# One block ahead: who writes the low parts of the expert weights in the selection stage

## What is computed

```python
q = (xb @ w_query).reshape(PEER_BLOCK, PEER_HEADS, 2, PEER_HALF)
s = jnp.einsum('bhpd,phnd->bhpn', q, sub_keys).astype(jnp.float32)
top_s, top_i = lax.top_k(s, PEER_TOPK)
cand = top_s[:, :, 0, :, None] + top_s[:, :, 1, None, :]
best_s, best_j = lax.top_k(cand.reshape(PEER_BLOCK, PEER_HEADS, PEER_TOPK * PEER_TOPK), PEER_TOPK)
...
eid = e1 * PEER_NKEYS + e2
gate = jax.nn.softmax(best_s, axis=-1)
act = jax.nn.gelu(jnp.einsum('bd,bhkd->bhk', xb, u_sel).astype(jnp.float32), approximate=False)
return jnp.einsum('bhk,bhkd->bd', (gate * act).astype(xb.dtype), v_sel)
```

## Time and profile before

| | us |
|---|---|
| median of 3 runs | 3571.84 (3567.01 to 3573.65) |
| profiled execution | 3573.65 |
| its span | 3572.0 |
| TensorE busy in the span (weight loads) | 3399.5 (3332.6) |
| VectorE busy | 2595.8 |
| ScalarE busy | 1021.5 |
| GpSimd busy | 978.6 |

### The profile page before, as it was taken

The page is one execution under the profiler, slowest core; times in us unless marked ns, Lnnn a source line. Parts: engine busy times, 40 slices in busy tenths (PEclk is TensorE's granted clock), DMA queues, the critical chain, the costliest instruction groups (busy, mean ns, idle before and its releaser), DMA issues.

```text
span 3572.0 us, 57535 instructions
## 1 busy us (share of the span) xinstructions
PE 3399.5 (95%) x21552; PEld 3332.6 (93%) x21552; DVE 2595.8 (73%) x5013; ACT 1021.5 (29%) x1355; POOL 978.6 (27%) x773
## 2 busy tenths in 40 slices
PE   6989999899998999999999899999999999999997
PEld 6989999879998999998898799999999999999996
DVE  5554344233343269999998999999999999999996
ACT  5742222121232233222454222222222222222222
POOL 0000000000000021111000655555555555555550
PEclk9999999879999999999999899999999999999998
DMA  2111111111232233333788999999899999989992
GB/s 107 36 34 37 47 39 37 49 48 47 76 119 75 84 102 113 104 106 105 218 266 275 358 322 327 338 329 322 322 327 328 334 331 326 325 319 332 326 325 108
DMA packets 304343, 698.60 MB, mean 196 GB/s; under 512 B 23856, under 2 KB 124208, under 8 KB 303184
## 3 DMA queue, kind: packets, MB, share of 16 engines
q0 software_dynamic: 98592, 362.97, 27.8%
q1 hardware_dynamic: 104112, 276.89, 22.6%
q10 hardware_dynamic: 101504, 56.89, 5.2%
HBM read 604.44 MB, written 92.22 MB: 195 GB/s over the span
## 4 chain that ended last, share of the span: by engine, by line
PE 78%; DVE 16%; DVEq 2%; issue 2%; DMA 1%; ACT 1%; ACTq 0%; POOL 0%; SPq 0%; PEldq 0%; POOLq 0%
PE PS L1454 28%; PE PS L366 16%; PE PS L1437 14%; PE PS L1158 7%; PE PS L1187 5%; DVE HOTG L1944 3%; PE PS L1369 3%; DVE HOT L1940 1%; PE PS L381 1%; DVE HOT L1941 1%; DVE fold L1872 1%; DVE besti L1816 1%; DVE sc L1807 1%; DVE besti L1808 1%; DVEq L1870 1%
## 5 line engine op out<-in xcount | busy, mean ns | idle before, releaser
L1454 PE MATMUL PS<-AH,VH 128*128 128x368 f32 x2048 | 515.5, 333 | 17.6 <-DVE AL L2042 12.6
L1454 PE MATMUL PS<-AH,VL 128*128 128x368 f32 x2048 | 516.4, 333 | 0.0
L1454 PE MATMUL PS<-AL,VH 128*128 128x368 f32 x2048 | 511.0, 331 | 0.0
L715 POOL DMA_INDIRECT SLOT<-rows_u,EID x256 | 346.9, 1355 | 598.4 <-DMA GW<-gate_matrices 293.0
L715 POOL DMA_INDIRECT SLOT<-rows_v,EID x256 | 333.2, 1301 | 203.4 <-DVE SLOT L1974 164.6
L1454 PEld LDWEIGHTS PS<-AH,VH 128*128 128x128 f32 x2048 | 366.5, 189 | 20.0 <-DVE AL L2042 13.5
L1454 PEld LDWEIGHTS PS<-AL,VH 128*128 128x128 f32 x2048 | 367.6, 189 | 0.0
L1454 PEld LDWEIGHTS PS<-AH,VL 128*128 128x128 f32 x2048 | 366.8, 189 | 0.0
L1983 DVE SCALAR_TENSOR_TENSOR XLF<-SLOT,GA,XLF 128x1024 f32<-128x1024 f32 x256 | 327.5, 1279 | 1.3 <-DMA SLOT<-rows_v,EID 1.1
L1044 ACT ACTIVATE VH<-VRAW 128x512 fp32r<-128x512 f32 x256 | 157.6, 628 | 567.2 <-PE PS L1454 567.2
L1974 DVE SCALAR_TENSOR_TENSOR SLOT<-SLOT,XHF 128x1024 f32<-128x1024 f32 x256 | 311.9, 1219 | 6.2 <-DMA SLOT<-rows_u,EID 6.2
(11 more groups left out here) (332 smaller groups left out, 6559.4 us busy)
## 6 DMA issues: line engine op xcount, KB each, us to landing
RAW<-experts_u SPq DMA_DIRECT2D x128, 512.0 KB, 6.0
VRAW<-experts_v SPq DMA_DIRECT2D x256, 256.0 KB, 5.7
gate_matrices<-stg ACTq DMA_DIRECT2D x22, 2048.0 KB, 10.3
GW<-gate_matrices SPq DMA_DIRECT2D x96, 384.0 KB, 6.8
RAW<-weights SPq DMA_DIRECT2D x69, 512.0 KB, 3.5
activations<-AS SPq DMA_DIRECT2D x64, 368.0 KB, 2.5
AS<-activations SPq DMA_DIRECT2D x64, 368.0 KB, 3.0
GW<-gate_matrices SPq DMA_DIRECT2D x32, 320.0 KB, 5.8
```

Source lines behind the costliest of these rows:

```text
L715: pool.indirect_dma_start(out=SLOT[n % NSLOT][:, :], out_offset=None, in_=table, in_offset=bass.IndirectOffsetOnAxis(ap=ids, axis=0)).then ...
L1454: mm = pe.matmul(PS[:, 4 + 2 * (d % 2) + t, 0:CH], w[:, d % 2, c * P:c * P + P], x[:, c, t * CH:t * CH + CH], start=(c == 0 and n == 0), s ...
```

## The change

GpSimd writes one more low part before tile 0 (blocks 0 to 3 in place of 0 to 2), and in the tiles +2, +3 and +4 in place of +1, +2 and +3. Its load of `qst` still stands behind the first of them. VectorE writes +5 and +6 in place of +4 and +5. Its first low part stands where it stood. The second stands ahead of the product with `second`, where it was behind it, and in the last tile there is none. The orders of TensorE, ScalarE and SyncE are the same as before.

```diff
-            for n in range(1, PRE + 1):
+            for n in range(1, PRE + 2):
                 e_low(n, n % 2)
...
-                e_low(FIRST_E[i] + 1, (FIRST_E[i] + 1) % 2)
+                e_low(FIRST_E[i] + 2, FIRST_E[i] % 2)
...
-                for r in range(2, SEL_E[i] - 1):
+                for r in range(3, SEL_E[i]):
                     e_low(FIRST_E[i] + r, (FIRST_E[i] + r) % 2)
...
                 dve.tensor_tensor(hot[:, :, :, :], places(topf), names(startb), ALU.is_ge)
-                e_low(FIRST_E[i + 1] - 1)
+                e_low(FIRST_E[i + 1])
...
                 dve.tensor_tensor(hot[:, :, :, :], places(topf), names(iota_b), ALU.is_equal)
+                if i + 1 < NTILE:
+                    e_low(FIRST_E[i + 1] + 1)
                 dve.drain()
                 dve.tensor_tensor(by_head(pick), by_head(hot), values(second), ALU.mult)
-                e_low(FIRST_E[i + 1])
                 fold(e2)
```

## The result

The change makes the kernel slower: 3619.51 us (median of 4 runs, 3618.04 to 3621.10) against 3572.52 for the kernel before on the same chip. The ratio is 1.0135, with a 95% interval of 1.0117 to 1.0152. That is 47.0 us more where 32.3 were forecast, and outside the range of 3588 to 3614. The direction and the place were right; the size was not.

What follows compares the result with a forecast made beforehand. VectorE's stream was taken as the clock from tile 2 on, TensorE in tiles 0 and 1. Terms 11.7 + 1.7 + 2.5 + 0.5 + 9.4 + 5.3 + 1.2 = 32.3 us gave 3604 us, range 3588 to 3614.

Steps and rivals of the forecast that it cites:

- steady tile: Tiles 4, 5 and 7: length from tick to tick grows from 47.65 to 50.9 us, taken as 3.15 a tile.
- rival 1: TensorE is the bound and its waits on VectorE's low parts go: about 3558 us; chance 4%.
- A: VectorE's early low-part place, L1781 after `hot` of L1877; forecast 3.25 us of new idle time before it in steady tiles.
- late place: VectorE's second low-part place in a tile; claimed to cost nothing more, with cover of 0.8 us a tile.
- block +3 ends at +32.75: TensorE, steady tile: start of scores to end of block +3 takes 19.70 us, so high part +5 is there at +35.9.
- lead in tiles 4 to 7: How far TensorE is ahead there; could be worse or better by 0.8 us a tile, ±3 in the sum.
- B: VectorE's late low-part place, reached at +45.3; high part +6 forecast near +44.5, 0.2 us of cost in tile 2.
- `qst` term: Tile 0: load queued behind GpSimd's first low part, so scores start at 1307.5 instead of 1304.40: 3.1 us of TensorE lost.
- Tile 6's growth: Tile 6 loses its short cast of `besti` (0.29 us) as the reason for 45.25 us and becomes about 50.6: 5.3 us.
- low part beside `hot`: GpSimd's low part +4 beside `hot` of L1877, 2.40 us alone, 2.55 beside VectorE's work: 0 to +0.8 in tiles 2 and 8.
- Rival 3: Only the early tiles pay; TensorE gets ahead after tile 3: 16.4 less 1.2 us, 3587; chance 10%.
- Rival 4: More than the sum: B's cover gone and `qst` late, 1 to 1.5 us more in each of eight tiles: 3615; chance 9%.

Runs made afterwards that it cites:

- fastest kernel of the study: Kernel before, but GpSimd writes +1 to +4, VectorE only +5 ahead of the product, and the exponential stands behind the fourth block: 3563.95 us.
- same kernel with the early exponential: Kernel before, but GpSimd writes +1 to +4 and VectorE only +5 ahead of the product; exponential left behind the third block: 3576.17 us.
- clock held: Changed kernel with useless matmuls in TensorE's wait before the scores: 3611.86 us; the 51.02 of tile 6 has them before block +4 too: 3610.29 us.
- first fillings: Changed kernel with useless matmuls on TensorE where it stands before the scores of tiles 1 to 8: 3611.86 us.
- both waits are filled: Changed kernel with useless matmuls on TensorE before the scores and also before the last block of a tile: 3610.29 us.

## Why the prediction was right and wrong

**Where it was right.** VectorE sets the pace in the steady tiles, and rival 1 (TensorE as the bound) fell: its waits for `WL` went away here, and the kernel is slower. The fastest kernel of the study has 1.22 us less on VectorE in each tile, and VectorE runs without a gap through its tiles 4 to 7; so it does in the same kernel with the early exponential, where the product of 3.2 us makes them 2 us longer. A waits nine times, seven of them for ScalarE's `WH` and two for GpSimd's low part +4 (4.5 us, tiles 2 and 8). The scores' starts (+13.03 forecast +13.05; in tile 0 1307.39 for 1307.5), the 3.03 us on ScalarE, the 14.9 us behind A in tile 5, and the free late place in tiles 4 to 6 all came as worked out. With the clock held, the steady tile is 50.99 for 50.9, and in the kernel with the change in tiles 4 to 8 only its first one is 50.95.

**The step that failed** is the 19.70 us from the start of the scores to the end of block +3 ("so block +3 ends at +32.75"). In tile 5 it took 22.5 us, to +35.6: from 1554.27 to 0.1 before ScalarE's table load at 1576.89. That duration was read where TensorE had come to the scores without a pause. The same paragraph puts a pause of 4 us in front of them, and behind it the scores took 6.09 us (tile 5), 5.0 (tile 4) and 4.95 (tile 0). The same happened in front of block +4 in tile 2, where TensorE stood 5.06 us. Filling the waits gave back 10.4 of the missing 14.7 us. The "lead in tiles 4 to 7" had a bound of ±0.8 a tile in the forecast; by the clock it was off by up to 2.8, which is why the range was missed too. The Trainium skill (page "TensorE: Matmul & The Clock Gate", section "HAM oscillation — how this bites in real kernels") says that a pause between groups of matmuls lets the clock fall, so that the next group begins at the low one. I had weighed no such case. The trace agrees in tile 5, 0.50 behind 4.06 us. How long the pause was doesn't settle it: it was 1.00 behind one of 3.69 us (tile 4 with the load of `qst` first) and 0.50 behind one of 1.82 us (tile 4 with the first fillings).

**The other terms.** Where both waits are filled, 4.3 us are still missing, in small pieces: tile 2 by 1.3, tile 3 by 1.0, tiles 0, 6, 1, 4, 5 and 7 by 0.2 to 0.5 each. In tiles 2 and 3 most of it is at B, which waits 0.93 and 0.68 us there where the forecast has 0.2 and nothing (1.09 and 1.08 with `qst` first as well): the late place was not free in them. The rest I have not taken apart. The `qst` term was 3.1 us in tile 0; the wait itself came out at 3.02, but with the clock it cost 4.9. Tile 6's growth was put down to its lost short cast, and with the clock held it is 51.02 as its neighbours are, so that reason stands. The low part beside `hot`, bounded by 0 to +0.8, took 2.91 to 3.01 us in seven of the eight tiles from 1 to 8, some 0.6 more than alone; the 2.55 us that the prediction names for it lie beside a cast. The lower end of the forecast's own sum is 32.3 - 0.6 - 3 = 28.7 and not 27, which changes nothing here, as the miss is above.

**Rivals.** Rival 3 (16.4 us, A no longer late after tile 3) is refuted by the kernel with the change in tiles 4 to 8 only, which loses 22.5 us there. Rival 4 had the nearest size (3615), with a mechanism that explains little of it: it has B wait in each of eight tiles, and B waited in three, 2.75 us in tile 2, 0.84 in tile 3 and 0.86 in tile 7. In tile 2 the filling took 1.8 of it away, and in tile 7 all.

## What to carry to other kernels

A wait put in front of TensorE where it ran densely can have two prices: its own length, and what the work behind it takes if the clock has fallen. So durations read where TensorE ran without a pause needn't hold behind a new one: here 3.3 us became 4.8 to 6.1 in five of nine cases. The row of the granted clock says which case it is, and the same trace can have both (here the scores of tiles 5 and 7). Before a producer's work is handed to another engine, ask how far ahead each asks for its input, and what stands in front of that input in an in-order queue: requests one block further ahead cost 47 us here. One low part a tile moved to GpSimd, with no request further ahead, cost 5, and won 8 once the exponential no longer stood before its split and the low part no longer met the product. When work moves to an engine, ask also what it will run beside there.

## What the runs showed that I had not expected

- Useless matmuls in a wait make the kernel faster: 23 in a tile, 4.0 us of TensorE's time, took the tile from 53.71 to 50.99 us.
- Pauses of 2.53 and 3.69 us left the clock at 1.00, and one of 4.06 was followed by 0.50 and 0.56 over the next 6 us. Of pauses of 1.82 and 1.84 us in the same kernel the first was followed by the low clock, which made its tile 1.3 us longer, and the second was not. One of 3.02 us (tile 0) made scores of 3.3 us take 4.95.
- Beside one GpSimd low part of 2.4 us, a cast of 0.29 us takes 2.33, five additions of 0.86 us take 2.56 and a product of 1.23 us takes 3.22, while the low part itself takes 2.39 to 3.12.
